# Picking the first expert's rows with one-hot products in a two-layer mixture-of-experts trunk

## What is computed

```python
scores = jax.nn.sigmoid((t @ w_router).astype(jnp.float32))
sel = scores + router_bias
grp = sel.reshape(-1, N_GROUPS, EXPERTS_PER_GROUP)
best_group = jnp.argmax(lax.top_k(grp, TOP_K)[0].sum(-1), axis=-1)
...
_, idx = lax.top_k(jnp.where(in_group, sel, -jnp.inf), TOP_K)
gate = jnp.take_along_axis(scores, idx, axis=-1)
gate = gate / jnp.sum(gate, axis=-1, keepdims=True)
hg = jnp.einsum('nd,edf->nef', t, wg)
hu = jnp.einsum('nd,edf->nef', t, wu)
act = jax.nn.silu(hg) * hu * combine[:, :, None]
out = jnp.einsum('nef,efd->nd', act, wd)
```

## Time and profile before

| | us |
|---|---|
| median of 3 runs | 1991.15 (1990.13 to 1992.47) |
| the profiled execution, its own time | 1984.46 |
| its span, first to last instruction | 1982.7 |
| PE matmul busy | 1869.7 (94%) |
| DVE busy | 1587.1 (80%) |
| ACT busy | 1431.7 (72%) |
| mean granted TensorE clock | 0.972 of full |

### The profile page before, as it was taken

One profiled execution on the slowest core, in us unless ns is written; L12 is line 12 of the kernel. 1 busy time (PEld: TensorE's weight loads), 2 busy tenths in 40 slices (PEclk: granted clock), 3 DMA queues, 4 the chain that ended last, 5 costly groups with the idle time before them and its releaser, 6 DMA issues.

```text
span 1982.7 us, 30643 instructions
## 1 busy us (share of the span) xinstructions
PE 1869.7 (94%) x9018; PEld 1507.4 (76%) x9018; DVE 1587.1 (80%) x2242; ACT 1431.7 (72%) x2279; POOL 86.2 (4%) x86
## 2 busy tenths in 40 slices
PE   7999999997999998989999999999889999998998
PEld 6887888886777777767778878888767777777775
DVE  5566777657999999989975667765689999998998
ACT  5465665446899888888755556664569988888895
POOL 0000000001000000000000000000010000000000
PEclk9999999997999999999999999999879999999999
DMA  7554444566999999999866444445579999999997
GB/s 276 200 187 150 149 165 156 192 226 224 399 404 414 404 404 405 405 387 418 336 221 232 149 170 154 166 149 203 211 269 397 410 406 417 408 404 394 393 422 265
DMA packets 82860, 582.08 MB, mean 294 GB/s; under 512 B 11662, under 2 KB 11918, under 8 KB 13166
## 3 DMA queue, kind: packets, MB, share of 16 engines
q1 hardware_dynamic: 75600, 542.01, 70.3%
q0 software_dynamic: 7168, 38.94, 5.7%
HBM read 575.91 MB, written 29.36 MB: 305 GB/s over the span
## 4 chain that ended last, share of the span: by engine, by line
PE 60%; DMA 16%; issue 8%; DVE 7%; ACT 7%; ACTq 0%; DVEq 0%; SPq 0%; POOL 0%; POOLq 0%
PE bank L867 11%; PE bank L869 11%; PE bank L868 11%; DMA raw<-in_expert_units 8%; DMA proj<-in_expert_units 7%; PE bank L1023 4%; PE bank L1025 4%; PE bank L1042 3%; PE bank L1044 3%; PE bank L1043 3%; ACT wh L582 2%; DVE wl L1223 2%; PE bank L1014 2%; DVE xl L1223 1%; PE bank L1006 1%
## 5 line engine op out<-in xcount | busy, mean ns | idle before, releaser
L1215 DVE TENSOR_TENSOR wl<-raw,wh 128x1024 fp32r<-128x1024 f32 x256 | 310.1, 1222 | 226.7 <-ACT wh L573 226.5
L573 ACT ACTIVATE wh<-raw 128x1024 fp32r<-128x1024 f32 x256 | 269.0, 1056 | 265.0 <-PE bank L869 262.8
L867 PE MATMUL bank<-wh,xh 128*128 128x512 f32 x1024 | 415.5, 406 | 2.3 <-DVE wl L1215 2.1
L869 PE MATMUL bank<-wh,xl 128*128 128x512 f32 x1024 | 401.9, 393 | 0.0
L868 PE MATMUL bank<-wl,xh 128*128 128x512 f32 x1024 | 400.6, 391 | 0.0
L1223 DVE TENSOR_TENSOR wl<-proj,wh 128x1024 fp32r<-128x1024 f32 x256 | 302.8, 1219 | 32.6 <-ACT wh L582 31.9
L1223 DVE TENSOR_TENSOR wl<-raw,wh 128x1024 fp32r<-128x1024 f32 x256 | 302.6, 1219 | 26.2 <-ACT wh L582 25.6
L582 ACT ACTIVATE wh<-proj 128x1024 fp32r<-128x1024 f32 x256 | 261.1, 1051 | 51.3 <-PE bank L1044 21.8
L582 ACT ACTIVATE wh<-raw 128x1024 fp32r<-128x1024 f32 x256 | 261.0, 1052 | 47.0 <-PE bank L1044 20.9
L1023 PE MATMUL bank<-wh,xh 128*128 128x512 f32 x648 | 271.0, 418 | 4.5 <-DVE xh L1664 3.0
L1025 PE MATMUL bank<-wl,xh 128*128 128x512 f32 x648 | 262.3, 405 | 0.0
(11 more groups left out here) (259 smaller groups left out, 2717.6 us busy)
## 6 DMA issues: line engine op xcount, KB each, us to landing
raw<-in_expert_units SPq DMA_DIRECT2D x192, 1024.0 KB, 15.8
proj<-in_expert_units SPq DMA_DIRECT2D x192, 1024.0 KB, 15.9
raw<-in_in_units SPq DMA_DIRECT2D x96, 1024.0 KB, 4.9
raw<-in_out_units SPq DMA_DIRECT2D x32, 1024.0 KB, 4.8
expert_rows<-rows POOLq DMA_DIRECT2D x4, 1024.0 KB, 4.5
proj<-picks POOLq DMA_DIRECT2D x4, 1024.0 KB, 7.8
x<-in_x SPq DMA_DIRECT2D x2, 1024.0 KB, 6.8
wide<-in_norms POOLq DMA_DIRECT2D x2, 1024.0 KB, 5.1
```

Of the source, the lines that this page charges most:

```text
L573: act_(wh[:, h % CUT, :], ring[j][:, h % 2 * HALF:(h % 2 + 1) * HALF], ACT.Copy)\
L867: mm(out, xh[:, at, tok], rh, start=start, stop=False)
L869: return mm(out, xl[:, at, tok], rh, start=False, stop=stop)
L1215: v.tensor_tensor(wl[:, h % CUT, :], ring[(first + h // 2) % slots][:, h % 2 * HALF:(h % 2 + 1) * HALF], wh[:, h % CUT, :].bitcast(F32), A ...
```

## The change

The first expert's rows aren't gathered any more. PE multiplies the normalised rows, which still lie in `rows`, by the first expert's one-hot matrix (`pick_rows`): 8 chunks of 128 features by 2 halves of the tokens in each of two groups, 32 products in all, each with a 128x128 piece of `rows` as the stationary side and 64 columns moving. The result already has the features on the partitions, so it takes the place of the transposes too. Since `rows` is overwritten by the experts' results, POOL reads it back from `rows_dram` at the end of every round (two DMAs of 1 MB), and PE's picks and ACT's first write of attention output wait for that; one small DMA at the program's start sets the count. Of the lists, those of experts 0 and 1 come before the picks, 2 to 5 behind them, 6 to 15 after halves 5, 6 and 7 of the first step. On DVE `rows_lo` moves from after cut 5 to after cuts 0 and 1, and `choose(EARLY, NE)` to after cut 2. PE turns the second expert's first group after half 6 in place of half 2.

```diff
-XT = {"mid": {PART + 3: 0, 2 * PART: 1}, "first": {2: 0, PART: 1}, "last": {}}
+XT = {"mid": {PART + 3: 0, 2 * PART: 1}, "first": {6: 0, PART: 1}, "last": {}}
...
+LISTED = {5: range(6, 9), 6: range(9, 12), 7: range(12, NE)}
+SECOND = PART // 2
...
@@ gpsimd
+            e.dma_start(small[0:1, :], small_in[0:1, 0, :]).then_inc(S["rows_back"], 16)
+            e.wait_ge(S["rows_back"], 16)
...
-                    gather(0)
                     gather(1)
...
                     e.wait_ge(S["out_ready"], t_.due("out_ready", NE - LAST))
+                    e.wait_ge(S["joined"], t_.due("joined", 4))
+                    e.wait_ge(S["x_cols"], t_.ahead("x_cols", 0) + 9)
+                    t_.fence()
+                    for t in range(NT):
+                        e.dma_start(rows[:, t, :], rows_dram[t * P:(t + 1) * P, :]).then_inc(S["rows_back"], 16)
@@ scalar
                 def output(i):
+                    if i == 0:
+                        e.wait_ge(S["rows_back"], t_.due("rows_back", 0) + 16)
@@ tensor
+            def pick_rows(g, m):
+
+                if g == 0:
+                    e.wait_ge(S["rows_back"], t_.due("rows_back", 0) + 16)
+                    e.wait_ge(S["xt_lo"], t_.due("xt_lo"))
+                for c in range(8):
+                    k = 8 * g + c
+                    for t in range(NT):
+                        last = mm(bank[m][:, c * SLOTS:(c + 1) * SLOTS], rows[:, t, k * P:(k + 1) * P],
+                                  chosen[:, t, 0, :], start=(t == 0), stop=(t == NT - 1))
+                last.then_inc(S["xt_banked"], 1)
...
             def step(b, kind):
                 for h, part in enumerate(PLAN[kind]):
                     n = PLAN[kind][:h].count(part)
+                    if h == SECOND and kind == "first":
+                        e.wait_ge(S["xt_lo"], t_.ahead("xt_lo", 1))
...
+                    if kind == "first" and h in LISTED:
+                        list_slots(LISTED[h])
                     if h in XT[kind]:
                         turn_gathered(1 - b, XT[kind][h])
...
+                e.wait_ge(S["rows_ready"], t_.due("rows_ready", NT))
                 with t_.one_round():
...
                     list_slots(range(FIRST))
+                    for g in range(2):
+                        pick_rows(g, (7, 5)[g])
                     list_slots(range(FIRST, EARLY))
-                    list_slots(range(EARLY, NE))
-                    for g in range(2):
-                        turn_gathered(0, g, (7, 5)[g])
                     e.wait_ge(S["xt_lo"], t_.due("xt_lo"))
-                    e.wait_ge(S["xt_lo"], t_.ahead("xt_lo", 1))
                     step(0, "first")
@@ vector
                         part_cut(h, at, kind)
-                        if h == DEEP_CUT - 1 and kind == "first":
-                            for g in range(2):
-                                rows_lo(0, g, (7, 5)[g])
+                        if h < 2 and kind == "first":
+                            rows_lo(0, h, (7, 5)[h])
+                        if h == 2 and kind == "first":
+                            choose(EARLY, NE)
...
                     tables(0, FIRST)
-                    choose(EARLY, NE)
                     step(0, "first")
```

More of the change, by code:

```diff
@@ L197 @@
     "joined": (0, 4), "x_ready": (2 * NT, 0), "x_cols": (4, 4), "sq_ready": (HA + HC, 0), "gains_ready": (1, 0), "rows_squared": (2, 0),
-    "rows_ready": (NT, 0), "rows_gained": (1, 0), "root_ready": (1, 0), "gain_free": (1, 0), "t_banked": (3 * NC // 2, 0), "t_hi": (3 * NC // 2, 0),
+    "rows_ready": (NT, 0), "rows_gained": (1, 0), "rows_back": (0, 16 * NT), "root_ready": (1, 0), "gain_free": (1, 0), "t_banked": (3 * NC // 2, 0), "t_hi": (3 * NC // 2, 0),
     "t_lo": (3 * NC // 2, 0), "qk_ready": (IN_UNITS // 4 - 1, 0), "f_hi": (1, 0), "f_lo": (1, 0), "f_banked": (1, 0), "f_ready": (1, 0),
```

## The result

| | us |
|---|---|
| median of 4 runs before, beside the changed kernel | 1990.64 (1979.19 to 1992.47) |
| median of 4 runs after | 2015.74 (2012.38 to 2019.36) |
| ratio of the runs, 95% interval | 1.0134 (1.0115 to 1.0154) |
| profiled execution after, its own time | 2013.57 |
| its span, against 1982.7 before | 2011.8 |

The change makes the kernel **slower by about 25 us**, with the sign as forecast; but 2015.74 lies above the range (1996 to 2010). Between the two profiled spans it is 29.1 us, where the sum had 14.1. Behind the experiments, one launch took 3297.93 us and one of the kernel before 6384.88, far from all the others, and the medians leave these two out.

The account below looks back on a forecast made before the run. Weight loads were taken to bound the expert stages, with DVE's cuts setting when they stream without a gap. 5.9 + 4.7 + 3.5 = 14.1 us slower took the median from 1991.15 to 2005.3 us, range 1996 to 2010.

Parts of the forecast that it names:

- the sum: Whole program: DVE's added waits of 5.9 and 4.7 us plus 3.5 for the last read-back, 14.1 us slower.
- PE's part: First list to half 0: picks at the low clock take 13.8 us, so half 0 starts 4.0 us later.
- DVE's part: Ahead of cuts 1 and 2: DVE waits 10.8 us for ACT's copies, delaying the layers by 5.9 and 4.7 us.
- I cost them at nothing: First step: the lists of experts 6 to 15 and the stacked pair fit beside DVE's cuts, 0 us.
- the bound: Tables after DVE's cut 12: if PE's lists were late, another 1 us per layer.
- The third rival: Layer 2's opening or the tables: read-back wait reaches PE, 3 us more, or late lists; 2008 to 2010, chance 0.07.
- The end: Program's end: the last read-back beside the output's stores adds 3.5 us, between 0 and 5.1.
- Layer 2's opening at nothing: Layer 1's read-back delays the `fcr` load, but 12.4 us and halves cut ahead hide it, 0 us.
- Nothing behind it takes it back: Expert stage: a DVE delay between 461 and 492 us delays the whole stage; a gain likewise.
- rival of a stage that absorbs the delay: Expert stages: loads have slack, so only the end pays, 3.5 us, giving 1994.7; chance 0.08.
- The first rival: Picks at full clock: 4.0 us gained over both layers, 1987.2 or 1990.7; chance 0.15, partly released clock included.
- The gather that is spared was hidden: Before half 0: PE never waits for the gather, so its removal gains nothing.

Follow-up runs that it names:

- the first experiment: The changed kernel with the second expert's first group turned after half 2 again, which also made PE wait for a later `rows_lo`: 2030.12 us, ratio 1.0211.
- all three causes taken away: The changed kernel with turn and its wait undone, 26 wide products, `rows_lo` behind cuts 2 and 4, `choose` behind cut 5, no layer 2 read-back: 1982.39 us, ratio 0.9969.

## Why the prediction was right or wrong

The sign was right and the size wrong: +14.1 us was the sum, +29.1 us the difference of the profiled executions, +25.1 that of the medians.

- **PE's part: right.** Picks of 13.8 us were foretold, 13.92 measured; half 0 16.5 and 16.6 us behind the first list. The choice of the low clock was the right one: the window 460 to 474 us shows 0.50 with PE busy for 14.00 of 14.00 us. With 20 wide products ahead the clock rose, and the same picks stayed at 1.00. The Trainium skill, page "TensorE: Matmul & The Clock Gate", section "Part 1: The HAM clock gate", says that sustained matmul activity releases the half clock. The wide products agree with that and these picks do not.
- **DVE's part: right in what it names.** 10.8 us of waits for the copies were foretold and 5.68 + 5.01 = 10.7 measured, which is +5.8 and +4.6 us against before.
- **"I cost them at nothing", of the lists and the turn moved into the first step: this step failed.** It left a delay of the ninth load of 11.9 - 5.9 = 6.0 us in layer 1 and 9.6 - 4.7 = 4.9 in layer 2 unaccounted for; in DVE's waits these are 1.05 + 5.10 us and 5.10 us. I had compared PE's time with DVE's cuts, and had asked when the tables get their lists; I was 1 us off there, as the bound said (1.05). But I had not followed the moved turn: it needs a `rows_lo` on DVE, this stands behind the tables, and PE, ACT and DVE queue behind each other from there. Moving the tables two cuts on takes back 5.7 and 2.6 us, moving the turn back 4.0 and 3.0. The turn was named in the account of the change, and no term was made of it. The same step took a half of PE "at full clock" as given: behind the moved lists the clock fell to 0.50 with PE busy, and in layer 2 of the run with the later tables the 2.3 us of the delay that were left went with it. Why it falls there, and in layer 1 of that run not, stays open.
- **The third rival** had "PE's late lists hold up the tables" at 2008 to 2010. It named the place but went only one step along the chain, to a price of 3 us, where the two layers together lose some 11.
- **The end: right in kind, too small.** I took 3.5 us between 0 and 5.1; 6.1 was measured, and the run without a read-back gives all of it back. A term was mis-sized here, not a mechanism wrong. The upper bound itself was too low. It was made of 2 x 2.54 us from the stream of weights, and beside the stores these 2 MB cost more. Here stores land after 9.9 us in place of 3.7. The Trainium skill, page "Trainium Kernel Development and Optimization", section "Key Constraints", says that DMAs of all queues run on the same 16 engines and interleave; that pointed to the right end of the range.
- **Layer 2's opening at nothing: right.** ACT's wait for `fcr` did come (5.33 us), and PE waited no longer for it. That halves cut ahead covered it, as the prediction had it, was not tested by itself. The +4.3 us of attention 2 in the profile goes for the most part with a spell of low clock that comes and goes between kernels with and without the read-back.
- **"Nothing behind it takes it back": right.** From the ninth load to the stage's end it is 493.0 and 497.9 us before, 492.2 and 497.0 after. Over the eleven runs it is 492.7 to 496.9 and 496.5 to 500.7, no shorter where the ninth load is late (494.4 and 499.0 in the first). So the rival of a stage that absorbs the delay is out.
- **The first rival, and the gather.** In the kernel after with full-clock picks the time was 2002.53, not under 1991, since this rival, too, left out the chain; with the chain and the last read-back gone too, the kernel with the picks is 5.8 us faster than the kernel before, and it then leaves out what a second round would need. "The gather that is spared was hidden" is true of the order before and stops being true once the lists move.

By terms, for the profiled spans: 21.5 in the openings (10.6 foretold, 10.9 not), 6.1 at the end (3.5 foretold), +4.3 and -1.1 in the two attentions, which no run ties to the change, and -1.7 behind the ninth loads: 29.1. Without the attentions it is 25.9, near the 25.1 of the medians.

What stays open: what lowers the clock inside the first step, why the wide products alone lower the median by 3 us when only one opening is earlier, and by 1.1 us, and whether the picks or the gather are better in time once both have the full clock. Reading the rows back in layer 2 only when another round follows, which would join the gain of 6 us with a program for lists of any length, wasn't tried.

## What to carry to other kernels

When a change moves a step past others on one engine, follow its partners on every other engine to the place where they now stand in the queue, and then what is queued behind whoever waits for them: here a turn moved by four halves made a chain of waits over PE, DVE and ACT; what it and the low clock behind it cost (10.9 us) is as much as the picks themselves (10.6), and one constant took back 8.3 us of it. A step that looks free because its wait is hidden (the gather) must be priced again in the new order, and a phase of narrow products on PE must be priced at the clock that the profile grants it. A transfer at the very end has no cover; leave it out or make it wait for the case that needs it.

## What the runs showed of the hardware

- **The 64-column products held the high clock, but did not raise it.** 64 picks without a gap ran at 0.50 for 13.92 us; behind 20 wide products (128x512, 7.45 us) and 6 more, the same 64 ran at 1.00 and took 7.36 us. In the kernel before with the same wide products the lists of four columns started quick (1.70 us for 24), but behind a wait of 1.16 us the clock fell in the lists that follow, and the 16 transposes were slow again (1.97 us).
- **The clock fell behind a stop of PE, and as well without one.** In the kernel after it is at 0.50 behind a stop of 4.34 us: the product behind it took 0.79 and the next 0.63 us, where 0.40 stands in the same kernel ahead of the stop (L1047, at 489.86 us). With the turn undone it fell at the same place with no stop (0.53 from 491 to 498 us, PE busy for 7.00 of 7.00), and with all three causes taken away too (0.50 from 481 to 487 us, 6.00 of 6.00). What PE did before, in all three, was lists of four columns between halves. But the same work does not always lower it: in the seven runs that have these lists in the step and no stop of PE over 1 us behind the first half, it fell in 8 of the 14 openings, in two runs in both layers, in four in one layer alone and in one in neither. With all three causes taken away layer 1, where it fell, has its ninth load 2.3 us behind that of layer 2, where it stayed at 1.00. In the two kernels with all lists ahead of the step it didn't fall inside the openings' steps at all.
- **Wide products did not always bring it back soon.** In the first experiment layer 1 stayed at 0.50 from 484 to 505 us with PE busy for 20.85 of 21 us, most of it in 128x512 products with lists and turns between them; in the kernel after it was back at 1.00 about 6 us behind the stop.
- **At the full clock a pick record takes 0.115 us**, 0.53 of the 0.217 at the low clock, and not the 0.101 of the row of the same shape that the prediction used.
- **2 MB read back beside 2 MB of stores cost some 6 us**: the seven traces with it have tails of 14.8 to 15.4 us, the six without 8.8 to 9.0. That is more than the 5.1 at which 2 MB of weights stream.
